# A gated decoder step on one core: merge gates spread over the two attentions, decay levels moved beside compression, norms by token tile

## What is computed

```python
q, kv6, ng, hq, hf, hi, hg, ga, gb = split(x @ w_in)          # ga, gb: the two merge gates, 1024 columns each
nsa_o = nsa(q, kv6, ng)       # compressed + selected + window attention; sample tokens read paged caches
hg_o  = hgrn2(hq, hf, hi, hg) # gated linear recurrence, 4 heads of 128
mix = (sigmoid(ga) * (nsa_o @ w_pa) + sigmoid(gb) * (hg_o @ w_pb)) @ w_o
h = layernorm(alpha * x + mix, ln1)
y = layernorm(alpha * h + moe(h), ln2)   # 32 experts, top 4 per token
```

## Time and profile before

| | us |
|---|---|
| three runs | 1651.17, 1652.79, 1656.56 |
| median | 1652.79 |
| the profiled execution: its own time | 1650.89 |
| its span, first to last instruction | 1649.1 |
| PE busy | 1455.6 (88%) |
| DVE, ACT, POOL busy | 431.8, 300.9, 80.5 |

### The profile page before, as it was taken

One profiled execution on the slowest core, in us unless ns is written; L12 is line 12 of the kernel. 1 busy time (PEld: TensorE's weight loads), 2 busy tenths in 40 slices (PEclk: granted clock), 3 DMA queues, 4 the chain that ended last, 5 costly groups with the idle time before them and its releaser, 6 DMA issues.

```text
span 1649.1 us, 20185 instructions
## 1 busy us (share of the span) xinstructions
PE 1455.6 (88%) x7423; PEld 654.3 (40%) x7423; DVE 431.8 (26%) x861; ACT 300.9 (18%) x545; POOL 80.5 (5%) x107
## 2 busy tenths in 40 slices
PE   6999988995755977999999999999999999999993
PEld 4757745574433624333333333323323323323321
DVE  0314432027422223221222212212212222222225
ACT  0103332014322012111111111111111111111111
POOL 0102300002000000000000000000000000000000
PEclk9999989997677996999999999999999999999997
DMA  6962120105155425999999999999999999999970
GB/s 235 335 212 103 32 77 23 29 22 175 33 165 151 160 92 233 420 417 417 418 416 418 419 414 418 418 417 418 417 415 418 412 405 419 409 405 419 410 313 30
DMA packets 116827, 476.52 MB, mean 289 GB/s; under 512 B 10451, under 2 KB 32275, under 8 KB 83827
## 3 DMA queue, kind: packets, MB, share of 16 engines
q1 hardware_dynamic: 112976, 465.78, 71.8%
q0 software_dynamic: 1856, 8.59, 1.5%
q10 hardware_dynamic: 1954, 1.63, 0.3%
HBM read 471.54 MB, written 8.59 MB: 291 GB/s over the span
## 4 chain that ended last, share of the span: by engine, by line
PE 49%; DMA 35%; DVE 8%; issue 2%; ACT 2%; SPq 2%; POOL 1%; DVEq 0%; ACTq 0%; POOLq 0%
DMA big<-in_w_gu 34%; PE bank L1027 14%; PE bank L688 7%; PE bank L633 5%; PE bank L1057 5%; PE bank L647 3%; PE bank L947 3%; PE bank L940 2%; PE bank L1013 2%; DVE big L433 1%; DVE work L1911 1%; PE bank L630 1%; DMA big<-in_w_in 1%; SPq L507 1%; SPq L508 1%
## 5 line engine op out<-in xcount | busy, mean ns | idle before, releaser
L1027 PE MATMUL bank<-big,gates 128*64 128x512 f32 x2048 | 451.1, 595 | 24.5 <-DMA big<-in_w_gu 23.7
L1027 PEld LDWEIGHTS bank<-big,gates 128*64 128x64 f32 x2048 | 142.1, 137 | 310.8 <-issue 257.1
L1057 PE MATMUL bank<-big,gates 128*64 128x512 f32 x1024 | 226.8, 595 | 0.0
L1911 DVE TENSOR_TENSOR work<-work,bank 128x512 f32<-128x512 f32 x198 | 127.0, 683 | 279.3 <-PE bank L1013 279.3
L1893 DVE TENSOR_SCALAR gates<-bank 128x512 f32<-128x512 f32 x32 | 22.1, 692 | 455.4 <-PE bank L1039 455.4
L1013 PE MATMUL bank<-gates 64*128 64x512 f32 x396 | 111.8, 641 | 21.0 <-DVE work L1911 21.0
L1057 PEld LDWEIGHTS bank<-big,gates 128*64 128x64 f32 x1024 | 70.7, 137 | 133.3 <-issue 133.3
L688 PE MATMUL bank<-big 128*128 128x417 f32 (+2 forms) x384 | 116.8, 464 | 4.6 <-DVE big L433 4.6
L1301 ACT ACTIVATE gates<-gates 128x512 f32<-128x512 f32 x32 | 20.2, 630 | 474.3 <-DVE gates L1893 474.3
L633 PE MATMUL bank<-xT,big 128*128 128x288 f32 x384 | 95.3, 407 | 0.0
L688 PEld LDWEIGHTS bank<-big 128*128 128x128 f32 x384 | 72.8, 191 | 46.5 <-issue 21.4
(11 more groups left out here) (336 smaller groups left out, 1163.4 us busy)
## 6 DMA issues: line engine op xcount, KB each, us to landing
big<-in_w_gu SPq DMA_DIRECT2D x128, 2048.0 KB, 23.1
big<-in_w_dn SPq DMA_DIRECT2D x128, 1024.0 KB, 21.2
big<-in_w_in SPq DMA_DIRECT2D x10, 2048.0 KB, 14.7
big<-in_cache_cmp_kv SPq DMA_DIRECT2D x64, 128.0 KB, 2.5
big<-in_cache_slc_kv SPq DMA_DIRECT2D x64, 128.0 KB, 2.1
big<-in_cache_win_kv SPq DMA_DIRECT2D x8, 512.0 KB, 3.6
big<-in_w_o SPq DMA_DIRECT2D x1, 4096.0 KB, 12.9
out_win_s<-in_cache_win_kv POOLq DMA_DIRECT2D x1, 4064.0 KB, 6.9
```

Source lines behind the costliest of these rows:

```text
L1027: last = pe.matmul(psum[2 + n][half * CAP:(half + 1) * CAP, :], xe[:, k % 4, (k // 4) * CAP:(k // 4 + 1) * CAP], gu_slot[k][:, c0:c0 + 512 ...
L1057: last = pe.matmul(psum[5][half * CAP:(half + 1) * CAP, :], act_T[:, k % 4, (k // 4) * CAP:(k // 4 + 1) * CAP], dn_slot[k][:, half * 512:( ...
L1911: dve.tensor_tensor(y, y, psum[6 + half][:, :], ALU.add).then_inc(y_added, 1)
```

## The change

The projection loses its 16 gate groups. They become `gate_group(f)`, called on PE at 16 places: eight in prompt attention (psum bank 4, copied by DVE), four in each half of sample attention (bank 6, copied by ACT). Each takes its 128 columns from one of eight loads of 256 columns, which SP puts into slots of `big` that are free at that time. A group waits until the one before it has been copied. The sigmoid over all gates stands behind the last.

```diff

 BLOCKS = [("kv", C_KV, 512, False), ("kv", C_KV + 512, KVW - 512, False), ("q", C_Q, 512, True),
           ("hf", C_HF, 512, True), ("hq", C_HQ, 512, True), ("hi", C_HI, 512, False),
-          ("hg", C_HG, 512, False), ("ga", C_GA, 512, True), ("ga", C_GA + 512, 512, True),
-          ("gb", C_GB, 512, True), ("gb", C_GB + 512, 512, True)]
...

-LEVEL_AFTER = [n for n, g in enumerate(GROUPS) if g[0] in ("ga", "gb")][1::2][:len(LEVELS)]
+LEVEL_AFTER = [GROUPS.index(("hi", 5, 0)), GROUPS.index(("hg", 6, 0)), GROUPS.index(("hg", 6, 2))]
...
+        wg_slot = [part(big, at, [KD, 2 * P]) for at in (8192, 10240, 8192, 10240, 20480, 22528, 8192, 10240)]
...
+            def load_gates(n):
+                sp.dma_start(wg_slot[n], ins["w_in"][0, :, C_GA + 2 * P * n:C_GA + 2 * P * (n + 1)].rearrange("(k p) n -> p k n", p=P))\
+                  .then_inc(w_loaded[1 + n % 2], 16)
+            sp.wait_ge(page_used, 6)
+            load_gates(0)
+            load_gates(1)
...
+            load_rows(0, 1)
+            sp.wait_ge(fill_done, 2)
+            load_gates(2)
+            load_rows(0, 2)
+            sp.wait_ge(fill_done, 4)
+            load_gates(3)
+            load_rows(0, 3)
+            for b4 in range(4):
+                if b4 % 2 == 0:
+                    sp.wait_ge(fill_done, 6 + b4)
+                load_window(0, b4)
             sp.wait_ge(pv_done, len(ITS))
+            load_gates(4)
+            load_gates(5)
+            sp.wait_ge(state_p_stored, 16)
+            load_rows(1, 2)
+            load_rows(1, 3)
             sp.wait_ge(states_stored, 16 * DB)
-            load_rows(1)
+            load_rows(1, 0)
+            load_rows(1, 1)
+            sp.wait_ge(fill_done, 12)
+            for b4 in range(4):
+                load_window(1, b4)
+            sp.wait_ge(spv_done, 1)
+            load_gates(6)
+            load_gates(7)
...
+            def gate_group(f):
+                pe.wait_ge(w_loaded[1 + f // 2 % 2], 16 * (f // 4 + 3))
+                pe.wait_ge(fill_copied, f + 1)
+                bank = psum[4 if f < 8 else 6]
+                for k in range(KD):
+                    last = pe.matmul(bank[:, 0:NT], wg_slot[f // 2][:, k, f % 2 * P:(f % 2 + 1) * P], xTv[:, k, :],
+                                     start=(k == 0), stop=(k == KD - 1))
+                last.then_inc(fill_done, 1)
...
             prompt_scores(0)
+            block_scores()
+            gate_group(0)
             prompt_scores(1)
+            gate_group(1)
             turn_outputs()
+            gate_group(2)
             for it in range(len(ITS)):
...
+                gate_group(3 + it)
+            gate_group(7)
...
+                gate_group(8 + 4 * s)
+                gate_group(9 + 4 * s)
...
+                gate_group(10 + 4 * s)
+                gate_group(11 + 4 * s)
```

```diff
+            for u in range(3):
+                turn_pages(u)
+                if u == 0:
+                    level_scores(3)
+                else:
+                    block_keys(2 * u - 1)
+                hidden(2 * u, 0)
+                if u == 0:
+                    level_scores(4)
+                hidden(2 * u, 1)
+                if u == 0:
+                    level_scores(5)
+                hidden(2 * u + 1, 0)
+                if u == 0:
+                    level_scores(6)
+                block_keys(2 * u)
+                hidden(2 * u + 1, 1)
...
+            def level_step(n):
                 dve.wait_ge(decay_ready, n)
                 dve.wait_ge(level_done, n)
                 dve.tensor_tensor(hqF[:, :, :], hq[:, :, :], hF[:, :, :], ALU.mult).then_inc(qf_ready, 1)
                 if n + 1 < len(LEVELS):
                     half_diff(n + 1)
                 add_level(n - 1)
-            add_level(len(LEVELS) - 1)
...
+            copy_units(0, 0, 6)
+            level_step(3)
+            copy_units(0, 6, 12)
+            level_step(4)
+            take_bias(0, 0)
+            level_step(5)
+            take_bias(0, 1)
+            level_step(6)
+            take_bias(1, 0)
+            last_level()
+            take_blocks(0)
```

```diff
+            def block_scores():
+                for it, (qt, hp) in enumerate(ITS):
+                    for hh in range(2):
+                        last = pe.matmul(psum[4][:, 4 * NCP * it:4 * NCP * (it + 1)].rearrange("p (g h c) -> p h g c", g=G, h=2)[:, hh, :, :],
+                                         qT[:, 0, 2 * hp + hh, qt * P:(qt + 1) * P], ckTp, start=True, stop=True)
...
+            def block_shift():
+                step = own.chain("pc_step", 0)
+                dve.wait_ge(pcs_step, 1)
+                mask = C("cmp_mask").rearrange("p (q c) -> p q c", q=2).unsqueeze(2).broadcast_to([P, 2, 8, NCP])
+                dve.tensor_tensor(pcs, psum[4][:, 0:16 * NCP].rearrange("p (q n c) -> p q n c", q=2, n=8), mask, ALU.add).then_inc(fill_copied, 1)
+                dve.wait_ge(fill_copied, 1)
+                step(dve.tensor_reduce(pc_stat[:, 0, :, :], pcs, AXX, ALU.max))
+                dve.tensor_tensor(pcs, pcs, pc_stat[:, 0, :, :].unsqueeze(3).broadcast_to([P, 2, 8, NCP]), ALU.subtract).then_inc(pcs_step, 1)
...
             prompt_max(0)
+            block_shift()
             prompt_max(1)
+            take_gates(0)
             outputs()
+            take_gates(1)
+            block_weigh()
             for it in range(len(ITS)):
                 prompt_weigh(it)
+                take_gates(2 + it)
                 if it + 2 < len(ITS):
                     prompt_max(it + 2)
                 else:
                     add_gain(it - 2)
                 prompt_out(it)
+            take_gates(6)
+            take_gates(7)
```

```diff
-            for i in range(6):
-                t0, m = TILES[i // 2]
+            for k in range(KD):
+                for c in range(4):
+                    last = pe.matmul(psum[4][NS * c:NS * (c + 1), 0:D // 4], mixT[:, k, SEQ:NT], w_o[:, k, c * D // 4:(c + 1) * D // 4],
+                                     start=(k == 0), stop=(k == KD - 1), skip_group_check=True)
+            last.then_inc(wo_done, 1)
+            def out_product(i):
                 for k in range(KD):
-                    last = pe.matmul(psum[(4 + i) % 8][0:m, :], mixT[:, k, t0:t0 + m], w_o[:, k, (i % 2) * 512:(i % 2 + 1) * 512],
...
+            LOGIT_BANK = (1, 4, 5)
+            out_product(0)
+            out_product(1)
+            turn_h(0)
+            out_product(2)
+            pe.wait_ge(router_loaded, 32)
+            router_product(0)
+            out_product(3)
+            pe.wait_ge(wo_done, 5)
+            pe.sem_inc(gu_free, KD // 2)
+            turn_h(1)
+            router_product(1)
+            turn_h(2)
+            router_product(2)
...
+            def norm_stats(rows, t, half):
+                m = TILES[t][1]
+                dve.bn_stats(ln_parts[0:m, t, half, :], rows[0:m, t, half * 512:(half + 1) * 512]).then_inc(own.next("ln_step"), 1)
+            def norm_scale(t, at):
+                m = TILES[t][1]
+                dve.wait_ge(own.semaphore, own.count)
+                dve.bn_aggr(ln_mean[0:m, t, :], ln_parts[0:m, t, :, :]).then_inc(own.next("ln_step"), 1)
+                dve.wait_ge(own.semaphore, own.count)
+                dve.tensor_scalar(ln_rstd[0:m, at % 3:at % 3 + 1], ln_mean[0:m, t, 1:2], LN_EPS, None, ALU.add).then_inc(ln_var, 1)
+            def norm_apply(rows, t, at, g, b, ready):
+                m = TILES[t][1]
+                rstd = ln_rstd[0:m, at % 3:at % 3 + 1]
+                dve.wait_ge(ln_rms, at + 1)
+                dve.reciprocal(rstd, rstd).then_inc(own.next("ln_step"), 1)
+                for half in range(2):
+                    cols = slice(half * 512, (half + 1) * 512)
+                    x = rows[0:m, t, cols]
+                    dve.scalar_tensor_tensor(out=x, in0=x, scalar=ln_mean[0:m, t, 0:1], in1=g[0:m, cols],
+                                             op0=ALU.subtract, op1=ALU.mult).then_inc(own.next("ln_step"), 1)
+                    dve.wait_ge(own.semaphore, own.count)
+                    dve.scalar_tensor_tensor(out=x, in0=x, scalar=rstd, in1=b[0:m, cols], op0=ALU.mult, op1=ALU.add).then_inc(ready, 1)
...
             dve.wait_ge(ln2_loaded, 32)
...
+                for half in range(2):
+                    y = y_rows[:, t, half * 512:(half + 1) * 512]
+                    dve.tensor_tensor(y, y, psum[LAST_BANKS[t] + half][:, :], ALU.add).then_inc(y_added, 1)
+                for half in range(2):
+                    dve.wait_ge(y_added, rounds * (6 * NE) + 7 + 2 * t + half)
+                    norm_stats(y_rows, t, half)
+                norm_scale(t, 3 + t)
+                if t:
+                    norm_apply(y_rows, t - 1, 2 + t, ln2[0], ln2[1], y_ready)
+            norm_apply(y_rows, 2, 5, ln2[0], ln2[1], y_ready)

```

648 lines of the change are left out of this document (348 added, 300 removed).

## The result

The changed kernel took **1559.24 us** (median of 4 runs, 1558.38 to 1560.08), the kernel before beside it 1654.67 (median of 4, 1651.17 to 1657.11). The ratio is 0.9425, 95% interval 0.9403 to 0.9446: 95.4 us faster, where 1571 and -79.5 had been forecast; the range of 1547 to 1598 holds it.

A forecast was written before the change was run, and what follows sets the result against it. DMA weight streaming bounds the expert loop from 652 us, PE's instruction list the time before it. Terms -73 + 17 + 4 - 7.5 - 16 - 4 = -79.5 take 1650.9 to 1571 us, range 1547 to 1598.

The forecast's parts named there:

- Projection and compression, -73: Start to first prompt scores: 73 us saved by removing gate groups and sigmoid and moving levels; bounds -79 and -60.
- Prompt attention, +17: Prompt attention: gate groups 0 to 7 and their copies add 17 us net; bounds +3 and +33.
- about 2 for scores that run at a higher clock: Prompt attention: about 2 us come back because scores run at a higher PE clock.
- Groups 6 and 7: End of prompt attention: two groups behind the last values, with a DVE copy between, delay the sample queries, 8.8 us.
- Sample attention, +4: Sample attention: groups add 20.2 us; 13 of row waiting and 3 from clock come back; bounds -4 and +17.
- Merge -7.5, LN1 and router -16: Before the expert loop: packed sample products save 7.5 us; only the last half tile's norm remaining saves 16.
- Experts 0: Expert loop: weight streaming stays unchanged, 943.0 us for 31 experts, 30.4 each.
- End, -4: After the last weight wait: DVE's reordered additions, statistics and norms take 19.5 us instead of 23.5; bounds -7 and 0.
- Warm clock: Rival in both attentions: filled gaps hold PE's clock up, costing 7 instead of 21 us; 1557 us, chance 0.17.
- Late rows: Rival in sample attention: SP's gate loads and waits between row loads keep the 13 us wait; 1584 us, chance 0.12.
- Cold groups: Rival in the attentions: PE at half clock makes ten of 16 groups cost 3.88 us more; 1610 us, chance 0.12.
- SP's queue: Slower rival: gate loads 2 to 7 delayed in SP's queue, up to 21 us each; 1697 us, chance 0.03.

The follow-up runs named there:

- before_thin: Kernel before the change, with one product of eight in each of its sixteen gate groups in the projection: 1649.53 us, ratio to before 0.9969.
- the three other profiles: Changed kernel with the second half's row loads after the state stores (1558.77 us), output stores issued by POOL (1565.30), or all six end additions first (1559.79).
- thin: Changed kernel with one product of eight in each gate group, the other seven left out: 1542.68 us, 16.6 faster than the changed kernel.
- norm_last: Changed kernel with DVE at the end making all six additions first, then the statistics, then the norms, instead of tile by tile: 1559.79 us.

## Why the prediction was right, and where its terms were off

The direction, the place of the gain and the order of its parts came out as forecast; the sum was 13 us short against the profiled execution, 16 against the medians. By the profiles, 2.8 of the 13 are the projection, 6.5 prompt attention and 5.0 the end. The loop started at 566.0, where 577 had been forecast.

*Projection and compression, -73:* -75.8. The landmark (149.6 against 150 to 153) and the wait of 5.40 for the level step are right; behind the first hidden product the stretch got 2.8 shorter instead of 1. But one reading behind the term fell. It booked 62.1 us as "16 groups on the path" because PE was busy for 76.05 of 77.00 us. With seven eighths of these products left out, before got only 4 us faster: under PE's full row lay the chain of the levels, 8.6 us a round. The sum was right since the change moves both, and the forecast had checked that the levels fit under hidden products. Had the change moved the groups alone, the same reading would have missed by some 50 us, if `before_thin` stands for that case.

*Prompt attention, +17:* +10.5 (+13.6 in the three other profiles). Up to the first turning the steps hold: 334.6 - 305.8 = 28.8 against 398.0 - 381.6 = 16.4, 12.4 more (11.5 forecast), though group 0 took 5.7 us, a part of them at half clock, not 3.88. From there to the last values it forecast +1 for groups and -2.3 and -2 for exponentials and clock, -3.3; measured -7.9 (-5.8 in the three others). The step that was off is "about 2 for scores that run at a higher clock": what grew faster was all of PE's work there, the transposes above all (421 ns to 273, medians). Groups 6 and 7: from the last values to the keys 11.4 us against 5.4, so 6.0, not 8.8; part of the two groups lies where PE already waited for the queries.

*Sample attention, +4:* +3.1. Half 1 took 43.7 instead of 35.5, half 2 40.4 instead of 32.6, so +8.2 and +7.8 (8.6 each by the forecast's 10.1 less half of 3), and the wait of 12.9 is gone. The size was right; of its reasons, the order of SP's waits is refuted, while PE's later place stands, together with states that are stored sooner.

*Merge -7.5, LN1 and router -16:* -8.5 and -16.2, which rest on the windows alone: no run takes either back. *Experts 0:* from the first issue to the last wait 943.1 against 943.0. The 2.8 us more lie ahead of it: the first pass of expert 0 took 16.67 us, before 13.95, after a stretch of 18.7 at 0.50. In the profile of every other changed version it took 13.95 or 13.96, so this is the clock at that moment and no cost of the change. But where PE's instructions were the same up to there, the attentions had taken 4 us more: the forecast of 21 for both is further from 13.6 than from 17.5, and a part of its miss is this one execution.

*End, -4:* -9.0. From the last wait to DVE's last pass 44.7 became 38.6, -6.1. The rest, -2.9, is the queue of the stores, which the forecast left at nothing although the change moves the stores from POOL to SP. DVE's part was sized at 3.8 + 3.8 + 2.1 + 9.0 and 0.8 of waits; it took 1554.30 - 1536.91 = 17.4 instead of 19.5. The statistics come 0.64 apart (0.68 long), inside the 0.5 to 0.8 given; the small instructions around them took about 0.4 a tile instead of 0.7, and the waits of 0.8 did not come.

*The rivals.* Warm clock gave 1557 and comes nearer than the forecast, by luck: it takes over the other terms of the forecast, and the projection and the end gained 7.8 us more than these. Its mechanism is borne out by thin (0.62 before, 1.00 after, 0.77 with thin groups), but its price (both attentions at +7; at the lower bounds that the prediction ties to it, -1) was too low: they cost 13.6 to 17.5, since the clock was high only behind the first turning, and groups 0, 1 and 9 met a PE at half clock. The prediction's reading that the clock is 1.00 where PE does not wait was too simple even for its rows: the last window of the earlier trace rows has PE busy for 8.10 of 8.20 us at 0.50. The Trainium skill, page "TensorE: Matmul & The Clock Gate", section "What's actually happening", has the slow clock as the default that sustained activity releases. Three windows agree, 0.62, 0.77 and 1.00 with PE busy for 68%, 72% and 86% of the stretch; a fourth, of `norm_last`, has 89% at 0.92, so the busy share alone doesn't order them. Late rows: no wait in after, but 4.3 us as soon as PE got there 12 us sooner, so that rival was near. Cold groups: three of sixteen (0, 1 and 9), and 13 too in the three other profiles. SP's queue: no group waited for its weights. So filled waits did raise the clock, which the prediction gave 0.17, and the groups still cost on the path, which it gave 0.55: both were true in part.

## What to carry to other kernels

A full row of PE doesn't say that PE's work is what sets the time: before booking a removed piece at its duration, follow the chain that runs beside it on the other engines (here masks, POOL, masks) and take the longer of the two. Independent products put into waits can cost far less than their time, as the work around them can run faster too, provided that each has a bank and a copy of its own to wait for; look at the engine that issues the loads next, because it gets to its limit as PE comes sooner. And before a stage of one profile is compared with a forecast to the microsecond, look at the same stage in a second run: here identical instructions took 165.0 and 169.0 us.

## What the runs showed of the hardware

With 62 us of products moved into two stages whose clock was 0.66 to 0.76, these took 13.6 to 17.5 us more in all (a wait of 12.94 for rows that went away counted in), and taking seven eighths of the products out again gave 17. A group of eight products took 4.1 us at 2.4 GHz; group 0 took 5.71 in one execution, its first 3.3 us at 0.52 and the rest at 1.00, and 6.59 in another with the same wait ahead. Group 13 took 4.12 and 5.81 behind the same wait of 3.02: the same instructions and waits don't always get the same clock. In the kernel before with thin groups the table load ahead of an exponential took 1.28 us (203.37 to 204.65), with the activation directly behind it at 204.66. `BATCH_NORM_STATS2` of 128 x 512 took 676 ns, the aggregation 204.
